# Another placement of the tensors in SBUF for a two-layer decoder trunk: a change of addresses alone

## The chip, the cores and the metric

The kernel runs on one core of a Trainium2 chip. Its time is that of one execution on the device, in microseconds; lower is better. PE is the matrix engine (TensorE), PEld its weight loads, DVE the vector engine, ACT the scalar engine, POOL GpSimd, and SP the engine whose queue issues nearly all DMAs.

## The reference

A trunk of two layers works on 512 tokens of 1024 features. Layer 0 mixes by differential attention (8 heads), layer 1 by causal pooling over 2, 4, 8 and 16 tokens. Each is followed by a convolutional gated MLP of width 2816 and a gated embedding. Everything is float32.

```python
def diff_attention(xn, w_qkv, ..., sub_g, w_o, lambda_init):
    q, k, v = jnp.split(xn @ w_qkv, 3, axis=-1)      # 8 heads, two 64-wide halves each
    ...
    a = jax.nn.softmax(jnp.where(causal, q @ k.T * ATTN_SCALE, -jnp.inf), axis=-1)
    o = (a[:, :, 0] - lam * a[:, :, 1]) @ v
    o = rmsnorm(o, sub_g) * (1.0 - lambda_init)
    return o @ w_o

def multiscale_pool(xn, w_pool, b_pool, scale):
    # per group g of 256 features: mean over the last POOL_WINDOWS[g] tokens, minus the token
    y = jnp.einsum('bsgc,gce->bsge', y, w_pool) + b_pool
    return y * scale

def conv_glu_ffn(xn, w_up, conv_w, conv_b, w_down):
    u = causal_depthwise_conv3(xn @ w_up, conv_w) + conv_b
    gate, up = jnp.split(u, 2, axis=-1)
    return (silu(gate) * up) @ w_down

def reference(...):
    h = x
    for i in range(2):
        h = h + (diff_attention, multiscale_pool)[i](rmsnorm(h, mix_norm_g[i]), ...)
        h = h + conv_glu_ffn(rmsnorm(h, ffn_norm_g[i]), ...)
        h = h + sigmoid(rmsnorm(h, ple_norm_g[i]) @ w_ple_gate[i]) * (p[i] @ w_ple_proj[i])
    return rmsnorm(h, final_norm_g)
```

## The kernel before

Features lie on the partitions and the 512 tokens along them, so one matmul has 128 x 128 weights and 512 moving columns. Each operand is held in two parts, a high one in the type fp32r (a rounded float32) and a low one that is what the high one leaves. A product is three matmuls into one PSUM bank: high by high, low by high, high by low (the helper `exact`, lines 1182 to 1184).

The weights come in units of up to eight 128 x 128 blocks. For a unit, SP loads `w_raw[s]` (512 KB, line 329), ACT rounds it into `w_hi[s]` (line 423, line 429 in attention), DVE writes the rest into `w_lo[s]` (line 781, line 787 in attention), and PE reads both. Three slots are in use in attention and four after it, so loading, splitting and multiplying of different units overlap. SP issues the load of a slot when DVE is done with the slot's last `w_raw`.

The moving operands are `x_hi`, `x_lo` (the input of the projections, of the up products and of the embedding's gate), `g_hi`, `g_lo` (the gated MLP values that the down products read; in the pooling layer they also hold the mixer's input and half of the product `z`, whose other half is `z0_hi`, `z0_lo`), `oT_hi`, `oT_lo` (attention's output), and `pT_hi`, `pT_lo` (the embedding's input). Inside attention they are `k_hilo` and `wT_hi`, `wT_lo`. At the start PE transposes `x_tok` and `p_tok`, which DMAs bring in; at the end ACT copies the transposed `y_gained` into `y_tok`, ACT and DVE scale it (lines 733 and 1172), and SP writes it out.

Each engine has its own program, written out in the order in which it runs. Every dependence is a semaphore that the text names: no wait is put in by an allocator or a scheduler from the tensors' places. The places follow from the text too: tensors are laid one behind the other in the order in which they are declared, and a scope (`ExitStack`) that is closed gives its space back to what is declared next. So tensors in two scopes share their space, and it is up to the semaphores that one is done before the other begins.

The numbers with an L below are lines of this kernel.

Of the kernel before, what the change touches and what calls it, by code (L numbers as in the profile page):

```python
# [8 lines left out]
F32 = mybir.dt.float32  # L9
F32R = mybir.dt.float32r  # L10
# [5 lines left out]
P = 128  # L16
D_MODEL = 1024
SEQ = 512
DEPTH = 2
N_HEADS = 8  # L20
# [3 lines left out]
PLE_DIM = 256  # L24
# [5 lines left out]
KT = D_MODEL // P  # L30
TT = SEQ // P
# [4 lines left out]
SLOTS = 4  # L36
UNIT_BLOCKS = KT
# [61 lines left out]
def hybrid_trunk(nc, x, p, mix_norm_g, w_qkv, lam_q1, lam_k1, lam_q2, lam_k2, attn_sub_g, w_attn_out,  # L99
                 w_pool, b_pool, pool_scale, ffn_norm_g, w_up, conv_w, conv_b, w_down,  # L100
                 ple_norm_g, w_ple_gate, w_ple_proj, final_norm_g, out):
    with ExitStack() as ctx:
# [3 lines left out]
        def sb(name, shape, dt, scope=ctx):  # L106
            return scope.enter_context(nc.sbuf_tensor(name, shape, dt))


        w_hi = [sb(f"w_hi{s}", [P, UNIT_BLOCKS * P], F32R) for s in range(SLOTS)]  # L110
        w_lo = [sb(f"w_lo{s}", [P, UNIT_BLOCKS * P], F32R) for s in range(SLOTS)]
        x_hi = sb("x_hi", [P, KT, SEQ], F32R)
        x_lo = sb("x_lo", [P, KT, SEQ], F32R)


        product = ExitStack()
        oT_hi = sb("oT_hi", [P, N_HEADS, SEQ], F32R, product)
        oT_lo = sb("oT_lo", [P, N_HEADS, SEQ], F32R, product)
        product.close()
        product = ExitStack()  # L120
        x_tok = sb("x_tok", [P, TT, D_MODEL], F32, product)
        p_tok = sb("p_tok", [P, DEPTH * TT, PLE_DIM], F32, product)
        product.close()
        product = ExitStack()
        y_tok = sb("y_tok", [P, TT, D_MODEL], F32, product)
        y_gained = sb("y_gained", [P, KT, SEQ], F32, product)
        product.close()
        g_hi = sb("g_hi", [P, KT, SEQ], F32R)
        g_lo = sb("g_lo", [P, KT, SEQ], F32R)
        xp_hi, xp_lo = g_hi, g_lo  # L130

        pT_hi = sb("pT_hi", [P, DEPTH * PLE_KT, SEQ], F32R)
        pT_lo = sb("pT_lo", [P, DEPTH * PLE_KT, SEQ], F32R)
        w_raw = [sb(f"w_raw{s}", [P, UNIT_BLOCKS * P], F32) for s in range(SLOTS)]
        h = sb("h", [P, KT, SEQ], F32)
        inv = sb("inv", [P, SEQ], F32)
        sq = sb("sq", [P, 2, SEQ], F32)

# [13 lines left out]


        start = ExitStack()
        par_rows = sb("par_rows", [P, 4, P], F32, start)
        lam_rows = sb("lam_rows", [HEAD_DIM, 8], F32, start)
        gain0_rows = sb("gain0_rows", [KT, P], F32, start)
# [2 lines left out]


        attn = ExitStack()
        CAUSAL = P * TT * (TT + 1) // 2
        probs = sb("probs", [P, 2, CAUSAL], F32, attn)
        wT_hi = sb("wT_hi", [P, CAUSAL], F32R, attn)
        wT_lo = sb("wT_lo", [P, CAUSAL], F32R, attn)
        k32 = sb("k32", [P, SEQ], F32, attn)


# [3 lines left out]
        vT = sb("vT", [P, SEQ], F32, attn)  # L173
        v_hi = sb("v_hi", [P, TT, P], F32R, attn)
        v_lo = sb("v_lo", [P, TT, P], F32R, attn)
        o32 = acc
        attn.close()


        ffn = ExitStack()  # L180
        emb = sb("emb", [P, KT, SEQ], F32, ffn)

        G = len(POOL_WINDOWS)
        band32 = sb("band32", [P, G, BAND], F32, ffn)
# [14 lines left out]
        z_hi, z_lo = (z0_hi, g_hi), (z0_lo, g_lo)  # L199
        ffn.close()  # L200


        bank = [ctx.enter_context(nc.psum_tensor(f"bank{b}", [P, SEQ], F32)) for b in range(8)]

# [1372 lines left out]
```

## Time and profile before

| | us |
|---|---|
| median of 3 runs | 1133.29 |
| the 3 runs | 1132.10, 1133.79, 1133.29 |
| the profiled execution | 1132.1 |
| its span, from the first to the last instruction | 1130.4 |
| PE busy in it | 1111.5 (98%) |
| DVE busy | 753.7 (67%) |
| ACT busy | 559.8 (50%) |
| DMA packets' time, as a share of 16 engines' span | 31% |

The three runs lie 0.15% apart. The page divides the span in 40 slices; PE is at 9 tenths or more in all but the first and the last. A matmul of 512 columns is shown with about 390 ns of busy time although the next one starts 227 ns after it, since matmuls are pipelined; what tells PE's pace is the distance of the starts.

### The profile page before, as it was taken

The page shows a single profiled execution, that of the slowest core. Times are in us where ns is not written, and L with a number is a line of the kernel's source. Part 1 is how long each engine was busy: PE and PEld are TensorE (multiplying, and loading weights), DVE is VectorE, ACT ScalarE, POOL GpSimd, SP SyncE. Part 2 cuts the span into 40 slices and gives each one's busy share as a digit, 9 for nine tenths or more (in the row PEclk, how much of TensorE's full clock was granted, in tenths as well). Part 3 has the DMA queues.
Part 4 walks back from the last instruction along what each step waited for, and adds up shares of the span by engine and source line. Part 5 has one row for each costly group of instructions (what it writes and reads, how often), then busy time and mean ns, then how long its engine had stood idle before and what let it go on. Part 6 is the DMA issues. An engine that isn't in the chain of part 4 may idle for free.

```text
span 1130.4 us, 14839 instructions
## 1 busy us (share of the span) xinstructions
PE 1111.5 (98%) x5201; PEld 924.4 (82%) x5201; DVE 753.7 (67%) x1080; ACT 559.8 (50%) x832; POOL 9.0 (1%) x57
## 2 busy tenths in 40 slices
PE   7999999999999999999999999999999999999996
PEld 6888888888888888888888888888888888888885
DVE  5878788765776347752676787777537774476773
ACT  7777776746554224431444577544314442244564
POOL 0000000002000000000000000000000000000000
PEclk9999999999999999999999999999999999999998
DMA  7232113132333423333323432133323333232411
GB/s 218 70 88 61 56 56 93 57 104 83 93 93 100 120 79 93 93 113 92 93 75 98 126 93 76 57 97 108 112 75 93 98 107 112 75 88 84 126 38 75
DMA packets 192544, 103.57 MB, mean 92 GB/s; under 512 B 3651, under 2 KB 190452, under 8 KB 192500
## 3 DMA queue, kind: packets, MB, share of 16 engines
q1 hardware_dynamic: 192484, 102.99, 30.9%
q8 instruction: 26, 0.43, 0.2%
q14 instruction: 18, 0.15, 0.0%
q10 hardware_dynamic: 16, 0.00, 0.0%
HBM read 100.89 MB, written 2.10 MB: 91 GB/s over the span
## 4 chain that ended last, share of the span: by engine, by line
PE 96%; ACT 1%; DMA 1%; DVE 0%; issue 0%; SPq 0%; ACTq 0%
PE bank L1182 30%; PE bank L1184 30%; PE bank L1183 30%; PE bank L1251 1%; PE bank L1253 1%; PE bank L1296 1%; DMA x_tok<-in_x 1%; PE bank L1278 1%; PE bank L1475 0%; PE bank L1270 0%; PE bank L1472 0%; PE bank L1207 0%; PE bank L1301 0%; PE bank L1302 0%; PE bank L1256 0%
## 5 line engine op out<-in xcount | busy, mean ns | idle before, releaser
L1182 PE MATMUL bank<-x_hi,w_hi 128*128 128x512 f32 x1024 | 400.9, 391 | 1.5 <-DVE h L798 1.5
L1184 PE MATMUL bank<-x_hi,w_lo 128*128 128x512 f32 x1024 | 399.3, 390 | 0.0
L1183 PE MATMUL bank<-x_lo,w_hi 128*128 128x512 f32 x1024 | 399.0, 390 | 0.0
L1182 PEld LDWEIGHTS bank<-x_hi,w_hi 128*128 128x128 f32 x1024 | 192.7, 188 | 41.3 <-issue 1.7
L1184 PEld LDWEIGHTS bank<-x_hi,w_lo 128*128 128x128 f32 x1024 | 192.5, 188 | 40.3
L1183 PEld LDWEIGHTS bank<-x_lo,w_hi 128*128 128x128 f32 x1024 | 192.7, 188 | 39.6
L423 ACT ACTIVATE w_hi<-w_raw 128x1024 fp32r<-128x1024 f32 (+1 forms) x166 | 169.5, 1027 | 102.9 <-PE bank L1184 102.9
L781 DVE TENSOR_TENSOR w_lo<-w_raw,w_hi 128x1024 fp32r<-128x1024 f32 (+1 forms) x166 | 198.0, 1194 | 33.7 <-ACT w_hi L423 33.5
L1182 PE MATMUL bank<-g_hi,w_hi 128*128 128x512 f32 x352 | 136.9, 389 | 0.0
L1183 PE MATMUL bank<-g_lo,w_hi 128*128 128x512 f32 x352 | 136.9, 389 | 0.0
L1184 PE MATMUL bank<-g_hi,w_lo 128*128 128x512 f32 x352 | 136.9, 389 | 0.0
L677 ACT ACTIVATE c<-u,params 128x512 f32<-128x512 f32 x88 | 71.9, 817 | 107.6 <-DVE u L1104 107.6
L1104 DVE TENSOR_TENSOR u<-bank,inv 128x512 f32<-128x512 f32 x88 | 60.7, 689 | 93.3 <-PE bank L1184 93.2
L1002 DVE TENSOR_TENSOR h<-bank,h 128x512 f32<-128x512 f32 x56 | 38.5, 688 | 97.9 <-PE bank L1184 97.9
L684 ACT ACTIVATE g_hi<-g 128x512 f32 (+1 forms) x44 | 27.8, 633 | 118.4 <-DVE g L1120 118.4
L1182 PEld LDWEIGHTS bank<-g_hi,w_hi 128*128 128x128 f32 x352 | 66.1, 188 | 13.7
L1183 PEld LDWEIGHTS bank<-g_lo,w_hi 128*128 128x128 f32 x352 | 66.1, 188 | 13.7
L1184 PEld LDWEIGHTS bank<-g_hi,w_lo 128*128 128x128 f32 x352 | 66.1, 188 | 13.7
L1114 DVE SCALAR_TENSOR_TENSOR c<-u,params,c 128x512 f32<-128x512 f32 x88 | 66.2, 752 | 9.7 <-DVE c L1109 0.9
L1109 DVE SCALAR_TENSOR_TENSOR c<-u,params,c 128x512 f32<-128x512 f32 x88 | 66.0, 750 | 2.3 <-ACT c L677 0.9
L682 ACT ACTIVATE s<-c 128x512 f32<-128x512 f32 x44 | 27.8, 633 | 74.6 <-DVE c L1114 74.6
L1122 DVE TENSOR_TENSOR g_lo<-g,g_hi 128x512 f32 (+1 forms) x44 | 30.5, 693 | 37.7 <-ACT g_hi L684 37.7
(196 smaller groups left out, 1116.1 us busy)
## 6 DMA issues: line engine op xcount, KB each, us to landing
w_raw<-in_w_up SPq DMA_DIRECT2D x88, 512.0 KB, 3.8
w_raw<-in_w_down SPq DMA_DIRECT2D x32, 512.0 KB, 3.5
w_raw<-in_w_qkv SPq DMA_DIRECT2D x24, 512.0 KB, 4.4
w_raw<-in_w_ple_gate SPq DMA_DIRECT2D x16, 512.0 KB, 3.5
w_raw<-in_w_down SPq DMA_DIRECT2D x16, 384.0 KB, 3.1
w_raw<-in_w_attn_out SPq DMA_DIRECT2D x8, 512.0 KB, 3.7
x_tok<-in_x SPq DMA_DIRECT2D x4, 512.0 KB, 5.3
w_raw<-in_w_ple_proj SPq DMA_DIRECT2D x4, 512.0 KB, 4.0
```

What stands on the lines that cost most here:

```text
L423: act.activation(w_hi[s][:, 0:w], w_raw[s][:, 0:w], ACT.Copy).then_inc(hi_done, 1)
L677: act.activation(c32[:, c, :], u32[:, c, PAD:PAD + SEQ], ACT.Identity, scale=tap(layer, 2, j + c * FT), bias=conv_bias(layer, j + c * FT)) ...
L682: act.activation(s32[:, :], c32[:, 0, :], ACT.Silu).then_inc(silu_done, 1)
L781: dve.tensor_tensor(w_lo[s][:, 0:w], w_raw[s][:, 0:w], w_hi[s][:, 0:w].bitcast(F32), ALU.subtract).then_inc(lo_done, 1)
L1002: dve.tensor_tensor(h[:, m, :], src, h[:, m, :], ALU.add).then_inc(evac_done, 1)
L1104: dve.tensor_tensor(u32[:, c, PAD:], bank[2 * v + c][:, :], inv[:, :], ALU.mult).then_inc(evac_done, 1)
L1109: dve.scalar_tensor_tensor(out=c32[:, c, :], in0=u32[:, c, PAD - 1:PAD - 1 + SEQ], scalar=tap(layer, 1, j + c * FT), in1=c32[:, c, :], op0 ...
L1114: dve.scalar_tensor_tensor(out=c32[:, c, :], in0=u32[:, c, PAD - 2:PAD - 2 + SEQ], scalar=tap(layer, 0, j + c * FT), in1=c32[:, c, :], op0 ...
L1122: dve.tensor_tensor(g_lo[:, 2 * a + v, :], g32[:, :], g_hi[:, 2 * a + v, :].bitcast(F32), ALU.subtract).then_inc(glo_done, 1)
L1182: pe.matmul(dst, w1, m1, start=start and i == 0, stop=False)
L1183: pe.matmul(dst, w1, m0, start=False, stop=False)
L1184: last = pe.matmul(dst, w0, m1, start=False, stop=stop and i == len(parts) - 1)
```

## The change

Tensors are declared in another order and in other scopes. No instruction, no wait, no size and no loop is touched. On every engine the two programs have the same instructions with the same waits in the same order (5,026 rows over all engines), if line numbers are left aside, which move by 6. Only the places of their operands along the partition differ, in KiB from its start:

| tensors | before | after |
|---|---|---|
| `w_raw` (4 slots) | 128.1 to 144.1 | 16.1 to 32.1 |
| `w_hi` | 16.1 to 32.1 | 32.1 to 48.1 |
| `w_lo` | 32.1 to 48.1 | 48.1 to 64.1 |
| `h` | 144.1 to 160.1 | 64.1 to 80.1 |
| `x_hi`, `x_lo` | 48.1 to 80.1 | 80.1 to 112.1 |
| `g_hi`, `g_lo`; `oT_hi`, `oT_lo`; `x_tok`, `p_tok`; `y_tok`, `y_gained` | 80.1 to 112.1 | 144.8 to 176.8 |
| `pT_hi`, `pT_lo` | 112.1 to 128.1 | the same |
| `inv`, `sq`, `diag`, `acc`, `params` and small ones | 160.1 to 176.8 | 128.1 to 144.8 |
| attention: `k32`, `q`, `k_hilo`, `vT`, `v` | 196.8 to 216.8 | 176.8 to 196.8 |
| attention: `probs`, `wT_hi`, `wT_lo` | 176.8 to 196.8 | 196.8 to 216.8 |
| `emb`, `band`, `u32`, `c32`, `s32`, `g32`, `z0_hi`, `z0_lo` | 176.8 to 216.8 | the same |

The end of the used space, 216.8 KiB, is the same. Modulo 64 bytes every tensor starts where it started. Modulo 256 bytes the group of `g_hi` moves: its first byte was 128 past a multiple, and is at one now.

```diff
--- before.py
+++ after.py
@@ -107,32 +107,14 @@
             return scope.enter_context(nc.sbuf_tensor(name, shape, dt))
 
 
+        w_raw = [sb(f"w_raw{s}", [P, UNIT_BLOCKS * P], F32) for s in range(SLOTS)]
         w_hi = [sb(f"w_hi{s}", [P, UNIT_BLOCKS * P], F32R) for s in range(SLOTS)]
         w_lo = [sb(f"w_lo{s}", [P, UNIT_BLOCKS * P], F32R) for s in range(SLOTS)]
+        h = sb("h", [P, KT, SEQ], F32)
         x_hi = sb("x_hi", [P, KT, SEQ], F32R)
         x_lo = sb("x_lo", [P, KT, SEQ], F32R)
-
-
-        product = ExitStack()
-        oT_hi = sb("oT_hi", [P, N_HEADS, SEQ], F32R, product)
-        oT_lo = sb("oT_lo", [P, N_HEADS, SEQ], F32R, product)
-        product.close()
-        product = ExitStack()
-        x_tok = sb("x_tok", [P, TT, D_MODEL], F32, product)
-        p_tok = sb("p_tok", [P, DEPTH * TT, PLE_DIM], F32, product)
-        product.close()
-        product = ExitStack()
-        y_tok = sb("y_tok", [P, TT, D_MODEL], F32, product)
-        y_gained = sb("y_gained", [P, KT, SEQ], F32, product)
-        product.close()
-        g_hi = sb("g_hi", [P, KT, SEQ], F32R)
-        g_lo = sb("g_lo", [P, KT, SEQ], F32R)
-        xp_hi, xp_lo = g_hi, g_lo
-
         pT_hi = sb("pT_hi", [P, DEPTH * PLE_KT, SEQ], F32R)
         pT_lo = sb("pT_lo", [P, DEPTH * PLE_KT, SEQ], F32R)
-        w_raw = [sb(f"w_raw{s}", [P, UNIT_BLOCKS * P], F32) for s in range(SLOTS)]
-        h = sb("h", [P, KT, SEQ], F32)
         inv = sb("inv", [P, SEQ], F32)
         sq = sb("sq", [P, 2, SEQ], F32)
 
@@ -152,6 +134,8 @@
 
 
         start = ExitStack()
+        x_tok = sb("x_tok", [P, TT, D_MODEL], F32, start)
+        p_tok = sb("p_tok", [P, DEPTH * TT, PLE_DIM], F32, start)
         par_rows = sb("par_rows", [P, 4, P], F32, start)
         lam_rows = sb("lam_rows", [HEAD_DIM, 8], F32, start)
         gain0_rows = sb("gain0_rows", [KT, P], F32, start)
@@ -160,10 +144,8 @@
 
 
         attn = ExitStack()
-        CAUSAL = P * TT * (TT + 1) // 2
-        probs = sb("probs", [P, 2, CAUSAL], F32, attn)
-        wT_hi = sb("wT_hi", [P, CAUSAL], F32R, attn)
-        wT_lo = sb("wT_lo", [P, CAUSAL], F32R, attn)
+        oT_hi = sb("oT_hi", [P, N_HEADS, SEQ], F32R, attn)
+        oT_lo = sb("oT_lo", [P, N_HEADS, SEQ], F32R, attn)
         k32 = sb("k32", [P, SEQ], F32, attn)
 
 
@@ -173,12 +155,19 @@
         vT = sb("vT", [P, SEQ], F32, attn)
         v_hi = sb("v_hi", [P, TT, P], F32R, attn)
         v_lo = sb("v_lo", [P, TT, P], F32R, attn)
+        CAUSAL = P * TT * (TT + 1) // 2
+        probs = sb("probs", [P, 2, CAUSAL], F32, attn)
+        wT_hi = sb("wT_hi", [P, CAUSAL], F32R, attn)
+        wT_lo = sb("wT_lo", [P, CAUSAL], F32R, attn)
         o32 = acc
         attn.close()
 
 
         ffn = ExitStack()
+        g_hi = sb("g_hi", [P, KT, SEQ], F32R, ffn)
+        g_lo = sb("g_lo", [P, KT, SEQ], F32R, ffn)
         emb = sb("emb", [P, KT, SEQ], F32, ffn)
+        xp_hi, xp_lo = g_hi, g_lo
 
         G = len(POOL_WINDOWS)
         band32 = sb("band32", [P, G, BAND], F32, ffn)
@@ -199,6 +188,11 @@
         z_hi, z_lo = (z0_hi, g_hi), (z0_lo, g_lo)
         ffn.close()
 
+
+        tail = ExitStack()
+        y_tok = sb("y_tok", [P, TT, D_MODEL], F32, tail)
+        y_gained = sb("y_gained", [P, KT, SEQ], F32, tail)
+        tail.close()
 
         bank = [ctx.enter_context(nc.psum_tensor(f"bank{b}", [P, SEQ], F32)) for b in range(8)]
```

## Rows read from the trace of the kernel before

**Rows 1.** The page: busy time of the engines, and the chain that ended last.

```profile
span 1130.4 us, 14839 instructions
...
PE 1111.5 (98%) x5201; PEld 924.4 (82%) x5201; DVE 753.7 (67%) x1080; ACT 559.8 (50%) x832; POOL 9.0 (1%) x57
...
PE 96%; ACT 1%; DMA 1%; DVE 0%; issue 0%; SPq 0%; ACTq 0%
```

**Rows 2.** The waits of PE: total us, times, longest us.

```profile
PE bank L1219 <- DMA x_tok<-in_x: 2.5, 2, 1.4
...
PE bank L1552 <- ACT sq L593: 1.5, 1, 1.5
```

**Rows 3.** The waits of the DMA queue on SP.

```profile
SPq L329 <- DVE w_lo L781: 776.4, 162, 17.3
```

**Rows 4.** Stretches: PE, PEld, DVE, ACT, POOL busy us (x instructions), granted clock, DMA share, GB/s.

```profile
60.00:80.00 20.00, 20.00 (x99) 16.21 (x99) 16.39 (x33) 15.18 (x32) 0.00 (x0) 1.00 0.11 32
300.00:800.00 500.00, 499.05 (x2293) 416.39 (x2292) 336.53 (x438) 227.34 (x298) 0.00 (x0) 1.00 0.32 94
```

**Rows 5.** PE by line and shape: total us, mean ns of one, idle before.

```profile
L1182 PE MATMUL bank<-x_hi,w_hi 128*128 128x512 f32 x1024 | 400.9, 391 | 1.5 <-DVE h L798 1.5
...
L1182 PE MATMUL bank<-g_hi,w_hi 128*128 128x512 f32 x352 | 136.9, 389 | 0.0
...
L1183 PE MATMUL bank<-wT_lo,v_hi 128*128 128x512 f32 x8 | 3.1, 390 | 0.0
...
L1472 PE MATMUL bank<-band,z_hi 128*128 128x144 f32 x8 | 2.0, 276 | 0.0
...
L1472 PE MATMUL bank<-band,g_hi 128*128 128x144 f32 x8 | 2.0, 274 | 0.0
```

**Rows 6.** Matmuls that read g_hi: duration min/median/max.

```profile
L1182 PE MATMUL bank<-g_hi,w_hi x352: 389/389/389, 358.2 to 1068.1; 128*128 128x512 f32 x176
```

**Rows 7.** Timeline of PE at 21 us: start, duration.

```profile
20.71 0.39 PE L1182 MATMUL bank<-x_hi,w_hi 128*128 128x512 f32 x1
...
25.47 0.39 PE L1182 MATMUL bank<-x_hi,w_hi 128*128 128x512 f32 x1
```

**Rows 8.** Timeline of PE at 372 us.

```profile
371.83 0.39 PE L1182 MATMUL bank<-g_hi,w_hi 128*128 128x512 f32 x1
...
373.19 0.39 PE L1182 MATMUL bank<-g_hi,w_hi 128*128 128x512 f32 x1
```

**Rows 9.** Timeline of PE at 80 us.

```profile
80.35 0.39 PE L1182 MATMUL bank<-wT_hi,v_hi 128*128 128x512 f32 x1
...
81.03 0.33 PE L1182 MATMUL bank<-wT_hi,v_hi 128*128 128x384 f32 x1
```

**Rows 10.** The load of p_tok, and its time to landing.

```profile
L360 SPq DMA_DIRECT2D p_tok<-in_p x1: 597/597/597, 18.6 to 18.6; - x1
...
DMA to landing us min/median/max: 5.9/5.9/5.9
```

**Rows 11.** A stretch of Rows 7, while p_tok lands.

```profile
22.00:24.00 2.00, 2.00 (x11) 1.65 (x10) 1.92 (x7) 1.98 (x4) 0.00 (x0) 1.00 1.07 350
```

**Rows 12.** DVE by line and shape.

```profile
L1058 DVE SCALAR_TENSOR_TENSOR z_lo<-bank,small,z_hi 128x512 fp32r<-128x512 f32 x4 | 3.0, 750 | 1.6 <-ACT z_hi L639 1.6
L1058 DVE SCALAR_TENSOR_TENSOR g_lo<-bank,small,g_hi 128x512 fp32r<-128x512 f32 x4 | 3.0, 749 | 1.8 <-ACT g_hi L639 1.8
```

**Rows 13.** ACT by line and shape.

```profile
L639 ACT ACTIVATE z_hi<-bank,small 128x512 fp32r<-128x512 f32 x4 | 2.8, 689 | 1.3 <-PE bank L1184 1.0 <-DVE small L824 0.2
L639 ACT ACTIVATE g_hi<-bank,small 128x512 fp32r<-128x512 f32 x4 | 2.7, 686 | 3.3 <-PE bank L1184 3.3
```

**Rows 14.** The chain in order of time: start, us, what.

```profile
2.68 8.44 DMA x_tok<-in_x
```

**Rows 15.** Timeline of PE at 16 us, at the low clock.

```profile
15.62 0.63 PE L1183 MATMUL bank<-x_lo,w_hi 128*128 128x512 f32 x1
16.04 0.63 PE L1184 MATMUL bank<-x_hi,w_lo 128*128 128x512 f32 x1
```


## Prediction, made before the changed kernel ran

> **What bounds the kernel now.** The page comes first: PE is busy for 1111.5 of 1130.4 us, and the chain that ended last is PE for 96% [rows 1]. So 1130.4 - 1111.5 = 18.9 us of the span are without a matmul, nearly all at its two ends. The waits of PE are next: at the start 2.5 us for the load of `x_tok`, at the end 1.5 us for the last square [rows 2]. In between nothing makes PE wait: the queue of loads waits for DVE to be done with a slot, 776.4 us in all, not PE for a load [rows 3], and the stretch from 300 to 800 us has PE busy for 499.05 of 500 us at full clock [rows 4]. Even in attention, where the other engines have most to do, DVE is busy for 16.39 and ACT for 15.18 of 20 us, PE for 20.00 [rows 4].
>
> So the time is the number of matmuls by their pace, and the question is whether the pace hangs on where the operands lie. The pace is read from the timeline: at 21 us two matmuls on `x_hi` start at 20.71 and 25.47 with 21 steps between them (every third reads `x_hi` with `w_hi`, and the rows between show 0.22 to 0.23 us each), so one step is 4.76 / 21 = 0.2267 us [rows 7]. Of 512 columns there are 3 x (1024 + 352) = 4128 on the `x` and the `g` operands [rows 5] (the other two lines of the product have the same counts): 4128 x 0.2267 = 936 us, or 83% of the span.
>
> **The change part by part.** *Instructions and waits*: none is removed, added or moved. Terms: 0. Since the waits are written by hand, sharing space with another tensor adds none either: `x_tok` and `oT_hi` shared their space before, and share it after.
>
> *PE's operands.* The three places that the trace before lets me compare are: `x` at 48 to 80 KiB with weights at 16 to 48, 0.2267 us a step [rows 7]; `g` at 80 to 112 KiB with the same weights, (373.19 - 371.83) / 6 = 0.2267 us [rows 8]; `wT` at 187 to 197 KiB as moving operand with `v` at 213 to 217 as weights, both above 128 KiB, (81.03 - 80.35) / 3 = 0.2267 us [rows 9]. The last pair has the place in the upper part that `g` gets now. A weight-side comparison is there too: the pooling layer loads `z_hi` at 200 KiB and `g_hi` at 80 KiB as weights for the same matmul, at 276 and 274 ns [rows 5]. The change moves `x` by 32, `w_hi` and `w_lo` by 16, `g` by about 65 KiB, all within what these rows span. Bounds: the mean durations differ by 391 - 389 = 2 ns between the `x` and the `g` lines [rows 5], which has other reasons in part (the first ones ran at the low clock); taken wholly as an effect of place on the 1056 matmuls that read `g`, it is 2.1 us either way. I take 0, as the steps are equal.
>
> *DVE and ACT.* Here the trace has an experiment of its own: the same instruction writes half of `z` to `z0` at 200 KiB and half to `g` at 80 KiB. DVE takes 750 and 749 ns [rows 12], ACT 689 and 686 [rows 13]. Even if all of DVE's 753.7 us [rows 1] grew by the larger relative difference, 3 of 686 or 0.4%, that is 3.3 us over the whole kernel, beside a PE that is fully busy; the cover in the densest stretch is 20.00 - 16.39 = 3.6 us in 20 [rows 4]. At the exposed ends, about 8 instructions of 0.7 us would carry it: 0.03 us. Cost 0.
>
> *The start.* The transposes wait for `x_tok`, whose last piece lands 8.44 us after its issue [rows 14]; it stands in the chain, so a faster or slower landing would be seen in full. Its destination moves from 80 to 145 KiB. The bounds are the waits there: at best PE's 2.5 us [rows 2] go, at worst the same again is added. I take 0: the issue, the size and what else is in flight are unchanged. The Trainium skill, "DMA: Bandwidth & Descriptors", section "How a descriptor splits into AXI transactions", speaks for a small gain: a descriptor that doesn't start at a multiple of 256 bytes begins with one transaction more. `x_tok` started 128 bytes past a multiple and starts at one now, so by an estimate from that page a row of 4096 bytes takes 16 transactions instead of 17, 6% of the landing or at most 0.5 us; the slots `w_raw` stay 128 bytes off and gain nothing. No row here shows the rule at work, and by it the sum would be 1132.7 instead of 1133.2.
>
> *The sum* against the profiled execution: 1132.1 (1130.4 of span and 1.7 around it) + 0 = 1132.1. That execution was the fastest of three; against their median of 1133.29 the same sum gives 1133.2, which I forecast.
>
> **The rivals.** *Slower: matmuls that are held up while DMAs land beside their operands.* Before, `w_raw` is written at 128 to 144 KiB and PE reads below 128; after, the landing slots lie right below `w_hi`, `h` lies between the weights and `x`, and `g` lies above. If landing or writing in the same part of the memory cost PE something, it would cost in the share of time in which DMA is active, 0.32 [rows 4], so on 0.32 x 4128 = 1321 matmuls. It decides from 2.3 / 1321 = 1.7 ns each. The 2 ns of rows 5 would give +2.6 us, 1135.9; as much again as the pace now has above the 512 / 2.4 = 213.3 ns of the full clock, 13.4 ns, would give +17.7 us, 1151, which is the time that I put beside this rival. Against it speaks the load of `p_tok`: it lands until 5.9 us after 18.6 [rows 10], at 96 KiB, in the low part where PE reads `x` and the weights; the 16 DMA engines were at a share of 1.07 and 350 GB/s at 22 to 24 us [rows 11], with ACT and DVE at 1.98 and 1.92 of 2 us, and the step was 0.2267 us all along [rows 7]. And the `g` matmuls, over 710 us in which everything else went on, have a least, median and greatest duration of 389 ns [rows 6]. The Trainium skill, "SBUF — State Buffer", section "Who interferes with whom", says the same: DMA never contends with a compute engine, and PE and ACT never wait on anyone. By that rule the rival has no way to act.
>
> *Faster: the pace has room that a better placement frees.* A step is 226.7 ns where the columns alone would take 213.3 at 2.4 GHz. If those 13.4 ns came from two operands getting in each other's way, and the new distance between them ended it, 4128 x 0.0134 = 55 us would go: 1078. The Trainium skill, "TensorE: Matmul & The Clock Gate", section "Wait — 56ns, not 53.3ns?", gives 215.7 ns for a warm matmul of 512 columns, so it leaves 11 of these ns unexplained. Against the rival: three different pairs of places have the same 226.7 [rows 7 to 9]; a conflict would hardly be the same in all of them.
>
> *That it does nothing at all* is not a rival but the forecast; what could feign an effect is the clock. The first projection ran at the low level of 1.2 GHz, 16.04 - 15.62 = 0.42 us a step [rows 15] against 0.2267, and how many matmuls that takes in may differ by some 6, or 6 x 0.2 = 1.2 us, either way, without the change having a part in it.
>
> **How the numbers follow.** No change 0.87. The landing rival 0.05, the faster pace 0.03, and some small effect of place that I have not named, beyond the 0.2% (2.3 us) which a measurement of this kernel can tell from no change, 0.03 faster and 0.02 slower. So faster 0.06, same 0.87, slower 0.07. The range: down to the fastest of before less the clock's 1.2 us, 1130.9; up to 1133.8, the slowest of before, plus the 2.6 us of the rival's small end, 1136.4.
>
> **What the profile after would show.** Right: the steps on `x_hi` and on `g_hi` are 0.227 us, the `g` line has 389 ns as least and greatest, DVE's and ACT's lines are within 3 ns of before, `x_tok` lands in about 8.4 us, PE is busy for about 1111 us. Wrong: a mean of the product's three lines above 392 ns with PE still at 98%, above all in stretches with much DMA (the landing rival), or steps of 0.215 us (the faster pace), or a longer first wait for `x_tok` by over 2 us.

## The result: 0.6% slower, in the matmuls that stream `g` and `oT`

The changed kernel takes 1140.32 us (median of 4 runs, 1139.62 to 1140.39), the kernel before 1133.54 (4 runs, 1132.10 to 1134.37). The ratio is 1.0062, with a 95% interval of 1.0050 to 1.0075. The forecast was no change, 1133.2 us, with a range from 1130.9 to 1136.4; the time lies outside it.

The page of the changed kernel (its lines of code are numbered 6 lower than before) answers to [rows 1]:

```profile
span 1137.8 us, 14839 instructions
...
PE 1119.3 (98%) x5201; PEld 924.7 (81%) x5201; DVE 753.4 (66%) x1080; ACT 559.7 (49%) x832; POOL 9.0 (1%) x57
...
PE 97%; ACT 1%; DMA 1%; DVE 0%; issue 0%; SPq 0%; ACTq 0%
```

The span is 7.4 us longer and PE is busy for 7.8 us more. DVE and ACT have what they had to within 0.3 us, 753.4 and 559.7 us. So nothing waits longer: the matmuls themselves go slower. Which ones, the view of PE by line and shape says, with total us, mean ns of one, and idle time before [rows 5]:

```profile
L1176 PE MATMUL bank<-x_hi,w_hi 128*128 128x512 f32 x1024 | 400.9, 392 | 1.5 <-DVE h L792 1.5
...
L1176 PE MATMUL bank<-g_hi,w_hi 128*128 128x512 f32 x352 | 139.0, 395 | 0.0
...
L1177 PE MATMUL bank<-oT_lo,w_hi 128*128 128x512 f32 x64 | 25.2, 394 | 0.0
...
L1177 PE MATMUL bank<-w_lo,g_hi 128*128 128x256 f32 x32 | 9.0, 282 | 0.0
...
L1177 PE MATMUL bank<-wT_lo,v_hi 128*128 128x512 f32 x8 | 3.1, 390 | 0.0
```

The matmuls on `x`, 3072 of the 4416 long ones in the projections and products, keep 390 to 392 ns. Those on `g` go from 389 to 395 ns, those on `oT` from 389 to 394. `wT` is unchanged, and so are those of 256 columns in which `w_lo` is streamed against `g_hi` as weights (282 ns in both traces). Where [rows 6] had 389 ns as least, median and greatest duration, the same view has now:

```profile
L1176 PE MATMUL bank<-g_hi,w_hi x352: 392/394/399, 358.3 to 1075.1; 128*128 128x512 f32 x176
```

The timeline shows the pace, to be held against [rows 8]; the first column is the start of each matmul in us:

```profile
372.27 0.40 PE L1176 MATMUL bank<-g_hi,w_hi 128*128 128x512 f32 x1
372.51 0.39 PE L1177 MATMUL bank<-g_lo,w_hi 128*128 128x512 f32 x1
372.74 0.40 PE L1178 MATMUL bank<-g_hi,w_lo 128*128 128x512 f32 x1
372.98 0.39 PE L1176 MATMUL bank<-g_hi,w_hi 128*128 128x512 f32 x1
373.20 0.40 PE L1177 MATMUL bank<-g_lo,w_hi 128*128 128x512 f32 x1
373.44 0.39 PE L1178 MATMUL bank<-g_hi,w_lo 128*128 128x512 f32 x1
373.67 0.40 PE L1176 MATMUL bank<-g_hi,w_hi 128*128 128x512 f32 x1
```

Six steps take 373.67 - 372.27 = 1.40 us, 0.2333 each instead of 0.2267, and two unequal steps alternate: 0.24, 0.23, 0.24, 0.22, 0.24, 0.23. The alternation goes through the line, whichever operand is high or low. Over 3 x 352 matmuls on `g` this is 1056 x 6.6 ns = 7.0 us, over 3 x 64 on `oT` it is 1.0 us, as the busy time of the three lines goes from 75.0 to 76.0 us: 8.0 us in all. What is missing to 7.4 stands at the start, in the chain of waits [rows 14], where the last piece of `x_tok` landed sooner in this execution:

```profile
2.68 7.40 DMA x_tok<-in_x
```

That is 1.0 us less than 8.44; 8.0 - 1.0 = 7.0 of 7.4 us are accounted for.

### The profile page after: what moved, and what is told of

Same layout as the page of the kernel before. It is cut to its first block, busy times and chain, and to the rows that moved or that the text cites. A ratio compares the mean times of both kernels' runs of the same rounds, so it can differ in the third digit from the quotient of the medians.

```text
span 1137.8 us, 14839 instructions
## 1 busy us (share of the span) xinstructions
PE 1119.3 (98%) x5201; PEld 924.7 (81%) x5201; DVE 753.4 (66%) x1080; ACT 559.7 (49%) x832; POOL 9.0 (1%) x57
## 4 chain that ended last, share of the span: by engine, by line
PE 97%; ACT 1%; DMA 1%; DVE 0%; issue 0%; SPq 0%; ACTq 0%
PE bank L1176 30%; PE bank L1178 30%; PE bank L1177 30%; PE bank L1245 1%; PE bank L1247 1%; PE bank L1290 1%; PE bank L1272 1%; DMA x_tok<-in_x 1%; PE bank L1469 0%; PE bank L1264 0%; PE bank L1466 0%; PE bank L1201 0%; PE bank L1295 0%; PE bank L1296 0%; PE bank L1250 0%
```

## Experiments

Two theories stood at first. *Phase*: the pace hangs on the distance between the start of the weights and the start of the moving operand, modulo some hundred bytes. Before, all are 128 past a multiple of 256; after, `g` and `oT` are at a multiple. *Parts*: it hangs on the weights lying below 128 KiB and `g` above it. No experiment changes an instruction or a wait; each only adds unused tensors ("gaps"), which shift what is declared behind them. "Before" in the ratios is the kernel before, measured beside each run on the same chip. e5 and e6 rest on 2 executions each, the others on 4 to 11.

| run | distance to the weights mod 256: x / g, oT | median us | ratio, 95% interval |
|---|---|---|---|
| e1, changed, g in phase, still high | 0 / 0 | 1133.36 | 0.9997 (0.9985 to 1.0009) |
| e2, before, g out of phase, still low | 0 / 128 | 1141.24 | 1.0069 (1.0050 to 1.0088) |
| e3, before, everything by 640 bytes | 0 / 0 | 1132.72 | 0.9993 (0.9982 to 1.0003) |
| e4, before, x by 128 | 128 / 0 | 1150.91 | 1.0157 (1.0136 to 1.0177) |
| e5, before, x by 64, g by 256, oT by 32 | 64 / 0, 32 | 1140.73 | 1.0069 (1.0044 to 1.0094) |
| e6, before, x by 32, g by 384, oT by 96 | 32 / 128, 96 | 1160.55 | 1.0244 (1.0218 to 1.0269) |
| e7, before, the weights by 128 | 128 / 128 | 1158.96 | 1.0227 (1.0206 to 1.0249) |
| e8, before, w_lo alone by 128 | 0 for w_hi, 128 for w_lo | 1151.15 | 1.0159 (1.0140 to 1.0179) |
| e9, changed, everything at a multiple of 256 | 0 / 0 | 1131.23 | 0.9991 (0.9982 to 1.0000) |
| e10, changed, stages by 128 | 0 / 0 | 1131.59 | 0.9989 (0.9979 to 0.9998) |
| e11, changed, stages by 256 | 0 / 128 | 1140.24 | 1.0063 (1.0048 to 1.0079) |
| e12, before, x_tok and p_tok by 128 | 0 / 0 | 1133.51 | 1.0002 (0.9992 to 1.0011) |

### Phase against parts: e1 to e4

e1 is the changed kernel with one gap:

```diff
+        pad_a = sb("pad_a", [P, 352], F32)
         start = ExitStack()
```

> The changed placement with 1408 unused bytes ahead of the stages' tensors, so that g, oT and all behind them still lie above 144 KiB, but start 128 bytes past a multiple of 2048 as the weights do. Theory of the phase (it matters where the moving operand starts against the weights, modulo some hundred bytes): about 1133.5 us, all steps on g back at 226.7 ns. Theory of the parts (it matters that the weights lie below 128 KiB and g above): stays at about 1140.3 us, steps on g alternate between 229 and 238 ns.

```profile
L1177 PE MATMUL bank<-g_hi,w_hi x352: 389/389/389, 358.2 to 1068.0; 128*128 128x512 f32 x176
```

The loss is gone, and the row above (least, median and greatest duration, as in [rows 6]) is at 389 ns again, with `g` still above 146 KiB and the weights below 65. The parts theory falls. e2 does the opposite in the kernel before:

```diff
+        pad_a = sb("pad_a", [P, 160], F32)
         product = ExitStack()
         oT_hi = sb("oT_hi", [P, N_HEADS, SEQ], F32R, product)
...
+        pad_b = sb("pad_b", [P, 352], F32)
         pT_hi = sb("pT_hi", [P, DEPTH * PLE_KT, SEQ], F32R)
```

> The placement before with 640 unused bytes ahead of g (and oT) and 1408 behind them, so that g stays below 128 KiB but starts 640 bytes out of phase with the weights, as in the changed kernel. Theory of the phase: about 1140.3 us, steps on g and oT of 229 and 238 ns. Theory of the parts: 1133.5 us, steps of 226.7.

```profile
L1184 PE MATMUL bank<-g_hi,w_hi x352: 392/394/398, 360.2 to 1077.1; 128*128 128x512 f32 x176
```

The whole loss is there with the weights, `g` and `oT` all below 113 KiB, in the same 392, 394 and 398 ns. e3 puts one gap of 640 bytes ahead of all:

```diff
+        pad_a = sb("pad_a", [P, 160], F32)
         w_hi = [sb(f"w_hi{s}", [P, UNIT_BLOCKS * P], F32R) for s in range(SLOTS)]
```

> The placement before with 640 unused bytes ahead of everything, so that weights, x, g and pT all start 768 past a multiple of 2048 and keep their distances. Theory of the phase, read as a distance between the two operands: 1133.5 us, all steps 226.7. Read as a place of the moving operand by itself (a start at a multiple of 256 bytes is slow): 4128 steps of 233.4 instead of 226.7, +28 us, 1161. Theory of the parts: 1133.5.

```profile
L1183 PE MATMUL bank<-g_hi,w_hi x352: 389/389/389, 356.5 to 1066.4; 128*128 128x512 f32 x176
```

`x` and `g` now start at a multiple of 256, as the slow `g` did, and are fast: it is the distance that counts, not the place of the moving operand by itself. e4 makes `x` slow instead of `g`, by 128 bytes:

```diff
+        pad_a = sb("pad_a", [P, 32], F32)
         x_hi = sb("x_hi", [P, KT, SEQ], F32R)
         x_lo = sb("x_lo", [P, KT, SEQ], F32R)
+        pad_b = sb("pad_b", [P, 480], F32)
```

> The placement before with 128 unused bytes ahead of x and 1920 behind it, so that only x is out of phase with the weights, by 128 bytes, and g is in phase. Theory of the phase with a period of 256 or 512 bytes: 3072 steps on x of 233.4 instead of 226.7 ns, +20.6 us, about 1154. If the period is longer than 512 bytes, 128 need not act as 640 does, and the time may stay at 1133.5. Theory of the parts: 1133.5.

```profile
L1185 PE MATMUL bank<-x_lo,w_hi 128*128 128x512 f32 x1024 | 405.2, 396 | 0.0
...
L1185 PE MATMUL bank<-g_lo,w_hi 128*128 128x512 f32 x352 | 137.0, 389 | 0.0
```

`x` goes from 390 to 396 ns, `g` keeps its 389, and the time rises by 17.0 us (forecast 20.6; 3072 x 6 ns of duration would be 18.4). Since 128 bytes do what 640 did, a pattern of 512 bytes or of a part of it fits both.

### How long is the pattern, and does an offset between help: e5, e6

Gaps of 64 and 192 bytes around `x`, 288 more ahead of `oT`, and 448 ahead of `pT` make e5; 32, 352, 224 and 288 make e6. A last gap ahead of `w_raw`, not shown, brings what lies behind back into its phase:

```diff
+        pad_x = sb("pad_x", [P, 16], F32)
         x_hi = sb("x_hi", [P, KT, SEQ], F32R)
...
+        pad_g = sb("pad_g", [P, 48], F32)
         product = ExitStack()
+        pad_o = sb("pad_o", [P, 72], F32, product)
         oT_hi = sb("oT_hi", [P, N_HEADS, SEQ], F32R, product)
...
+        pad_p = sb("pad_p", [P, 112], F32)
         pT_hi = sb("pT_hi", [P, DEPTH * PLE_KT, SEQ], F32R)
```

> The placement before with small unused gaps, so that against the weights x starts 64 bytes out of phase, g 256, oT 32 and pT 192 (before: 0 for all). If the pattern repeats every 256 bytes, g keeps 226.7 ns a step; if every 512 or more, g is slow as at 128 (233.4). For the offsets between: if the loss grows with the offset up to 128, x at 64 has about 230 ns a step and the time is +10 us, about 1144; if every offset that is no multiple of 256 costs the same, x has 233 ns, +20 us, about 1154. A theory by which 226.7 ns is itself a clash that some offset avoids expects a step nearer to 213 ns for one of the four.

```profile
L1187 PE MATMUL bank<-x_hi,w_hi 128*128 128x512 f32 x1024 | 405.2, 396 | 0.8 <-DVE h L803 0.8
L1189 PE MATMUL bank<-x_hi,w_lo 128*128 128x512 f32 x1024 | 402.3, 393 | 0.0
L1188 PE MATMUL bank<-x_lo,w_hi 128*128 128x512 f32 x1024 | 399.0, 390 | 0.0
...
L1188 PE MATMUL bank<-g_lo,w_hi 128*128 128x512 f32 x352 | 137.0, 389 | 0.0
...
L1188 PE MATMUL bank<-oT_lo,w_hi 128*128 128x512 f32 x64 | 25.3, 395 | 0.0
...
L1188 PE MATMUL bank<-pT_lo,w_hi 128*128 128x512 f32 x32 | 12.6, 395 | 0.0
```

`g` at 256 is fast: the pattern repeats every 256 bytes. `oT` at 32 and `pT` at 192 are slow too (before, these two lines had 389 and 391 ns). `x` at 64 loses less, and unevenly: 396, 390 and 393 ns by line. Its three lines are busy for 1206.5 us in all, against 1199.2 before and 1217.2 in e4, so 64 bytes cost about 0.4 of what 128 do.

> As the run before it, with x 32 bytes out of phase, g 384, oT 96 and pT 160. A period of 256: g at 384 is slow as at 128, 233.4 ns a step, +7 us. Loss growing with the offset: x at 32 about 228.3 ns, +5 us, in all about 1145. Same loss for every offset: x 233 ns, +20, in all about 1161.

```profile
L1188 PE MATMUL bank<-x_lo,w_hi 128*128 128x512 f32 x1024 | 404.9, 395 | 0.0
...
L1188 PE MATMUL bank<-g_lo,w_hi 128*128 128x512 f32 x352 | 139.0, 395 | 0.0
...
L1188 PE MATMUL bank<-oT_lo,w_hi 128*128 128x512 f32 x64 | 25.4, 397 | 0.0
...
L1188 PE MATMUL bank<-pT_lo,w_hi 128*128 128x512 f32 x32 | 12.7, 395 | 0.0
```

`x` at 32 and `g` at 384 (128 modulo 256) lose the full 5 to 6 ns; `oT` at 96 loses 4 to 8 ns by line and `pT` at 160 loses 4 to 5. So neither guess on the shape was right: the loss doesn't grow with the offset, since 32 costs what 128 does, and is not the same for all, since 64 costs less than half. No offset gave a line of these products a mean duration under 389 ns, so none of them frees any of the 13.4 ns above 213.3.

### Which of the two operands, and when: e7, e8

e7 moves both parts of the weights by 128 bytes and leaves the rest in its phase; e8 moves `w_lo` alone:

```diff
+        pad_0 = sb("pad_0", [P, 32], F32)
         w_hi = [sb(f"w_hi{s}", [P, UNIT_BLOCKS * P], F32R) for s in range(SLOTS)]
         w_lo = [sb(f"w_lo{s}", [P, UNIT_BLOCKS * P], F32R) for s in range(SLOTS)]
+        pad_1 = sb("pad_1", [P, 480], F32)
         x_hi = sb("x_hi", [P, KT, SEQ], F32R)
```

> The placement before with the weights w_hi and w_lo moved by 128 bytes and 1920 unused bytes behind them; x, g, oT, pT, w_raw and h keep their phase. Theory of the distance between weights and moving operand: all 4416 matmuls of 512 columns in the projections and products are slow, 233.3 instead of 226.7 ns, +29 us, about 1163. Rival (it is the moving operand's distance from what DMA, ACT or DVE touch, w_raw or h, which moved along in the run with everything shifted): 1133.5.

```profile
L1185 PE MATMUL bank<-x_lo,w_hi 128*128 128x512 f32 x1024 | 405.2, 396 | 0.0
...
L1185 PE MATMUL bank<-g_lo,w_hi 128*128 128x512 f32 x352 | 139.0, 395 | 0.0
...
L1185 PE MATMUL bank<-oT_lo,w_hi 128*128 128x512 f32 x64 | 25.3, 395 | 0.0
...
L1185 PE MATMUL bank<-pT_lo,w_hi 128*128 128x512 f32 x32 | 12.6, 395 | 0.0
```

`x`, `g`, `oT` and `pT` are all slow, though none of them moved against `w_raw` or `h`, and the time is 24.9 us longer (forecast 29). The rival (the distance to what DMA, ACT or DVE touch) falls.

> The placement before with w_lo alone moved by 128 bytes; w_hi, x, g, oT, pT and w_raw keep their phase. Theory that a weight load clashes with the matmul that streams meanwhile: one load in three (that of w_lo, beside the matmul of the low part with w_hi) is out of phase, so about a third of the loss, +10 us, about 1143, and the steps are unequal by line. Rival (the matmul clashes with its own weights or the loss hangs on the moving operand alone): also a third or nothing, but in the line of high by low.

```profile
L1186 PE MATMUL bank<-g_hi,w_lo 128*128 128x512 f32 x352 | 139.8, 397 | 0.0
L1185 PE MATMUL bank<-g_lo,w_hi 128*128 128x512 f32 x352 | 139.4, 396 | 0.0
L1184 PE MATMUL bank<-g_hi,w_hi 128*128 128x512 f32 x352 | 137.0, 389 | 0.0
```

Here my theory was too narrow. High by low is slow (397 ns), in which the moving operand is out of phase with the weights in use while `w_hi`, in phase, is loaded for the next. Low by high is slow too (396), in which it is the other way round. Only high by high, where both are in phase, has 389. So two steps of three lose, and 17.1 us are 0.69 of e7's 24.9. That either the weights in use or those being loaded will do is one reading of this, but it isn't shown: a lost step can't be pinned on the pair of its own record. e4 shows it where `x`, out of phase, gives way to `g`, in phase with all weights:

```profile
364.23 0.39 PE L1184 MATMUL bank<-g_hi,w_hi 128*128 128x512 f32 x1
...
364.93 0.39 PE L1184 MATMUL bank<-g_hi,w_hi 128*128 128x512 f32 x1
...
365.61 0.39 PE L1184 MATMUL bank<-g_hi,w_hi 128*128 128x512 f32 x1
```

The first three matmuls on `g` still take 0.70 us, 0.233 a step, and the next three 0.68, 0.227. So a step can be slow although the operands of its own record are in phase, and one out-of-phase part may be enough for both slow lines of e8.

### The smallest repair, a control, and the start: e9 to e12

```diff
+        pad_a = sb("pad_a", [P, 32], F32)
         start = ExitStack()
```

is e10; e11 has 64 in place of 32; e9 has the line of e10 and the same gap ahead of `w_raw`, the first tensor.

> The changed placement with 128 unused bytes ahead of the stages' tensors: the smallest edit that brings g and oT into phase with the weights modulo 256 (both 128 past). Distance modulo 256: about 1133.5, g at 226.7 ns a step. If the pattern needs 512 or 2048 bytes, g is 768 off modulo 2048 and 256 off modulo 512, and stays slow in part or in full, up to 1140.3.

```profile
L1177 PE MATMUL bank<-g_hi,w_hi x352: 388/389/390, 357.5 to 1067.3; 128*128 128x512 f32 x176
```

> The changed placement with 256 unused bytes ahead of the stages' tensors, a control: everything in the stages moves, the distance modulo 256 stays 128. Distance modulo 256: about 1140.3, steps of 229 and 238 ns on g. If any gap there undoes the loss (by what it moves otherwise), 1133.5.

```profile
L1177 PE MATMUL bank<-g_hi,w_hi x352: 392/394/398, 358.9 to 1075.8; 128*128 128x512 f32 x176
```

A gap of 128 bytes takes the loss away, one of 256 leaves it whole: it is not the gap but what it does to the distance modulo 256.

> The changed placement with 128 unused bytes ahead of everything and 128 more ahead of the stages' tensors, so that weights, x, g, oT, pT and x_tok all start at a multiple of 256. Theory of the distance modulo 256 bytes between weights and moving operand: every step 226.7 ns. If x_tok lands sooner at a multiple of 256 (7.1 to 8.1 us in the four traces with such a start, 8.1 to 8.8 in the six others), another 0.8 us go: about 1132.7. If that is chance, 1133.5. By the theory of the parts (weights low, g high) it would be 1140.3.

e9 came out at 0.9991 of before, e10 at 0.9989. They are the lowest medians measured here, but only about a thousandth from the kernel before, and e10, with `x_tok` still at 128, is no worse than e9. Part even of that thousandth is the clock's: in 7 of their 11 executions each the mean granted clock was 0.995 or more, in 10 of 27 of the kernel before, and such executions of the kernel before took 1131.7 us on average, the others 1133.8. Neither placement is shown to beat the kernel before by more than the 0.2% of the prediction.

> The placement before with x_tok and p_tok alone moved by 128 bytes, to a multiple of 256. If the start of a landing's rows at a multiple of 256 matters: the last piece of x_tok lands after about 7.6 us instead of 8.4 and the time is 0.8 us shorter, about 1132.7. If not: 8.4 us, 1133.5.

```profile
2.68 8.40 DMA x_tok<-in_x
```

`x_tok` and `p_tok` alone are at a multiple of 256 here; `x_tok` lands after 8.40 us, as before, and the time is 1.0002 of before. Over all profiles the landing took 7.1 to 8.4 us with such a start and 7.5 to 8.8 with the other, so the 1.0 us that the changed kernel gained there is within what it varies by. The means of seven profiles each are 7.8 and 8.3 us, which these spreads don't tell apart.

## Why the prediction was wrong

- **Nothing is added, no wait arises, PE alone sets the time**: right. PE waits for `x_tok` as long as before, DVE's and ACT's times are the same.
- **PE's operands, "I take 0, as the steps are equal"**: this step failed. The three pairs of places that I compared differed in their region, from 16 to 217 KiB, but not in their phase: `x` and `g` with the weights are 128 and 128 modulo 256, and `wT` and `v`, both 768 past a multiple of 2048, are 0 and 0. The change moved `g` against the weights by 640 bytes modulo 2048, and no long matmul of the trace before was out of phase. The comparison couldn't show what it was used to rule out. In place of the 0 the runs showed 6.6 ns a step on `g` and about 5 on `oT`, 8.0 us. The text under the table of the change even gave the number, that the first byte goes from 128 past a multiple of 256 to one; I used it for the DMAs alone.
- **The comparison with `z_hi` and `g_hi` as weights** (276 and 274 ns) did hold one pair out of phase, but at 144 columns. The changed trace has the 256-column matmuls out of phase at the same 282 ns. So short ones don't show the loss, and they were no evidence for long ones.
- **The bound from the durations**, 2 ns or 2.1 us on the 1056 matmuls of `g`, was too tight by a factor of three: 6.6 ns, 7.0 us. `oT` was left out, 1.0 us more.
- **The landing rival** named the right side and the right engine, but the wrong cause: e1 loses nothing with the landing slots and `h` where the change put them, e2 loses the same with them within 2 KiB of where they were, and e7 loses it everywhere, likewise. Its sign, a mean above 392 ns with PE still at 98%, did appear, on `g` and `oT` alone. Its chance of 0.05 covered none of what happened; that was the 0.02 for an effect of place that I had not named.
- **The faster rival**, that the 13.4 ns above 213.3 are a clash that another distance ends: wrong at all seven distances modulo 256 that were tried (0, 32, 64, 96, 128, 160 and 192).
- **The start**: the rule that I drew from the Trainium skill, "DMA: Bandwidth & Descriptors", section "How a descriptor splits into AXI transactions", gave up to 0.5 us. e12 shows 0.04 us at the landing and a time that is 0.9 us shorter to 1.2 us longer, too wide to tell 0.5 us. The packet records of the traces tell more. The 512 rows of `x_tok`, written into SBUF, take 156 ns at least and 159 in the median in all 14 traces, wherever they start. The 512 rows of `y_tok`, read out of SBUF at the end, take 159.0 to 159.1 ns on average in the six traces where it starts at a multiple of 256 bytes, and 163.8 to 164.0 in the eight where it starts 128 past one. So a cost of the start shows where SBUF is read, not where it is written, and I had put it on the written side.
- **"PE and ACT never wait on anyone"**, from the Trainium skill, "SBUF — State Buffer", section "Who interferes with whom": that holds between engines as far as these runs go. The same section calls PE's two read ports, one for the moving operand and one for the weights, independent; here the distance between what the two read sets the pace, 226.7 or 233.3 ns.
- **Two sizes**: the sum against the median of 1133.29 gives 1133.3, not 1133.2. The clock's 1.2 us was small too: the kernel before took 1131.7 us on average with a mean granted clock of 0.995 or more and 1133.8 below it (the 27 executions beside e9 to e12), about 2 us apart.

Open: the mechanism inside PE or the memory. The runs show that the distance modulo 256 bytes between moving operand and weights decides, that 0 is free, that 32, 96, 128, 160 and 192 cost 4 to 7 ns in a step of 226.7, and that 64 costs about 0.4 of what 128 does. They don't show why, nor which of the two reads is held up. 96, 160 and 192 were tried on `oT` or `pT` alone, and only the type fp32r was.

## What to carry to other kernels

Where matmuls of 512 columns in fp32r run back to back, each with new weights, let the weights and the moving operand start at the same distance from a multiple of 256 bytes; an odd tensor of 640 bytes declared between them costs as much as 3% of every long matmul, and no wait in any view shows it. Compare the mean and the least, median and greatest duration of the same matmul between two placements, and before calling two places equal, write down both addresses modulo 64, 128, 256 and 512, not only their region. A natural comparison in a trace rules out only what differs between its two sides.

## What the runs showed of the hardware that I had not expected

- A long matmul's step depends on the distance of its two operands: 226.7 ns in phase, 233.3 on average out of phase by 128 bytes, in the changed kernel as an alternation of about 0.23 and 0.24 us. It goes on whatever DMA, ACT and DVE do: all 352 matmuls of the `g_hi` line have 392 to 399 ns, over 717 us.
- With one of the two weight parts out of phase, two steps of three are slow (e8: 396 and 397 ns beside 389), and after a run out of phase the next three matmuls, in phase, are still slow (e4: 0.233 us a step, then 0.227).
- Rows of 4096 bytes read out of SBUF by DMA take 164 ns from a start 128 past a multiple of 256 and 159 from a multiple; rows written to SBUF take 159 in the median from either.
- Matmuls of 256 columns with the same offset show nothing (`w_lo` against `g_hi`: 282 ns in both placements).
